# State-space mixer: one decay matmul for four heads, the gate, the root and the low parts a slot later, and four blocks begun at the end

## The chip, the core and the metric

The kernel runs on one core of one Trainium2 chip. The metric is the time of one execution in microseconds of device time. Before the change three runs gave 1684.92 us as median (1684.12 to 1685.75).

## The reference

Two transformer-like stacks run one behind the other on 256 tokens of width 1024 (16 meta tokens in front make it 272 in the first stack). The change touches the first layer alone, the state-space mixer. Cut to that:

```python
def ssd_mixer(h, w_in, conv_w, conv_b, dt_bias, a_log, d_skip, norm_g, w_out):
    zxbcdt = h @ w_in
    z, xbc, dt = jnp.split(zxbcdt, [SSD_D_INNER, SSD_D_INNER + SSD_CONV_DIM], axis=-1)
    xbc = jax.nn.silu(causal_depthwise_conv(xbc, conv_w, conv_b))
    xs, b_in, c_in = jnp.split(xbc, ...)
    dt = jax.nn.softplus(dt + dt_bias)
    ...
    a_cs = jnp.cumsum(a_dt, axis=-1)
    decay = jnp.exp(jnp.where(causal, a_cs[..., :, None] - a_cs[..., None, :], -jnp.inf))
    cb = jnp.einsum('bclgn,bcsgn->bcgls', c_c, b_c)
    y_diag = jnp.einsum('bcgjls,bcsgjp->bclgjp', cb[:, :, :, None] * decay, xdt)
    ...   # states carried from chunk to chunk, y_off from them
    y = y + xs * jnp.repeat(d_skip, SSD_HEAD_DIM)
    g = (y * jax.nn.silu(z)).reshape(bsz, L, SSD_GROUPS, SSD_D_INNER // SSD_GROUPS)
    g = g * lax.rsqrt(jnp.mean(g * g, axis=-1, keepdims=True) + EPS)
    return (g.reshape(bsz, L, SSD_D_INNER) * norm_g) @ w_out
```

There are 32 heads of 64 in 8 groups of 4, a state of 128, and a convolution of 4 taps. Behind the mixer come its MLP, an attention layer with its MLP, and the second stack; they are the same in both kernels.

## The kernel before, in words

All weights pass through as blocks of 128 output channels, in the order of one list, `PLAN`. Of each block of 128 x 1024 numbers SyncE loads the raw float32 (`RAW`, four slots), ScalarE makes the high part (`WH`, `act_split`), VectorE subtracts it to get the low part (`WL`, `dve_split`), and TensorE multiplies: for each of 8 chunks three matmuls, high by high, high by low, low by high (`pe_chunks`). A slot of `WH` is free again when TensorE has finished the block four places before. ScalarE splits three blocks ahead, VectorE two.

The mixer has 48 input blocks, six for each head group: two of x, one of B, one of C, two of the gate z. The code of each engine is written out in the order in which it runs: for each block n there stand the block's own work (split, convolution, SiLU) and then the steps of head groups that are due, which `ssd_cores` gives as pairs (g, k) with k = n - 6g - 5. So k counts the block at which a step of group g is issued, and one table, spread over `pe_ssd_core`, `act_ssd_core`, `dve_ssd_core` and `pool_ssd`, decides on every engine what is done at which k. For a convolved block ScalarE makes the base (scaled by tap 3, plus bias), VectorE adds three taps from the PSUM bank, ScalarE makes the tanh, and VectorE the SiLU from it.

A group is worked on in three tiles of tokens, 16, 128 and 128 wide. For each there are:

- `pe_prepare`: the product of B and C, transposes, and the running decay sums of the four heads laid over all partitions. The latter are four matmuls with a selector column (`DSEL`) as broadcast weights and the decay rows (`ACS`: 32 rows of high parts, 32 of low ones) as moving operand.
- `act_prepare`: exponentials of the sums (`CE`, for the part from the carried state) and of the differences (`EE`), and a copy of B transposed.
- GpSimd (`pool_ssd`): `CE` times C, in place, for tiles 1 and 2. It is the only GpSimd work of a round.
- `dve_prepare`, `dve_weigh`, `pe_apply`, `dve_take`: the masked product, the weighting by the decay, the products with x and the state, the sum with the skip term.

When the three tiles are through, the group is gated (VectorE, one instruction over 544 elements), squared (ScalarE), summed over channels (TensorE, `pe_group_sums`, two matmuls with ones), and its root is taken: ScalarE makes a rough one by logarithm and exponential, which needs a load of another function table and a load back (`act_table`), and VectorE corrects it by three Newton instructions (`dve_newton`). VectorE multiplies, ScalarE makes the high parts (`ASH`, `act_part`) and VectorE the low parts (`ASL`) which the output projection reads.

In the output projection (`ssdo`) row 0 takes chunks of groups 0 to 3 and row 1 those of groups 4 to 7, in 8 blocks each. While group 7 is still being worked on, `pe_ssd` begins the first three blocks of row 1 with the six chunks that are ready, and finishes them when group 7's low parts are there.

A name like pb stands for all PSUM banks, SCR for one large scratch tile in which most of the mixer's tiles are carved out. Below stand the functions that the change touches.

Of the kernel before, what the change touches and what calls it, by code (L numbers as in the profile page):

```python
# [22 lines left out]
for _n, _w in [("eps", 1), ("one", 1), ("lnmix", 16), ("ones", 128), ("ident", 128), ("tri", 128), ("convw", 128),  # L23
               ("convb", 32), ("dtb", 1), ("dsel", 32), ("alog", 1), ("ssdd", 16), ("ssdn", 16), ("lnmlp", 16),
               ("m384", 384), ("again", 384), ("past", 128), ("cmask", 128), ("sel2", 142), ("bdm", 128),
               ("i384", 1), ("i256", 1), ("rsel", 16), ("cs", 272), ("onerow", 256),
               ("qan", 3), ("kvan", 2), ("qn", 1), ("kn", 1), ("kn1", 1), ("memn", 8), ("ng", 96), ("gatb", 1),
               ("hg", 8)]:
    COLS[_n] = (_at, _w)
    _at += _w  # L30
# [171 lines left out]
def build_program(nc, cpack, xin, memin, W, out):  # L202
    with ExitStack() as ctx:
# [9 lines left out]
        def sig(name):  # L213
            sigs.append(Sig(sem(name)))
            return sigs[-1]
# [91 lines left out]
        def bank_of(i):  # L307
            name, r, m = PLAN[i]
            if name == "wqb":
                return banks[m // 2 % 2]  # L310
            return banks[3 if name == "mlao" and m == 3 else MEMBANK.get((name, m), i % 3)]

# [7 lines left out]
        def pe_bank_free(q, i):  # L320

            name, r, m = PLAN[i]
            if name == "wqb":
                if m > 3:
                    if m % 2 == 0:
                        q.wait_ge(*qsq[m // 2 - 2])
                else:
                    q.wait_ge(*eva[AT["wk", 0, 7]])
            elif name == "mlao" and m < 3:
                q.wait_ge(*qsq[7])  # L330
                q.wait_ge(*kw[15])
            elif name == "mlao" and m == 3:
                q.wait_ge(*ex[14])
            elif AT["ssd", 0, FIRST] <= i - 3 <= AT["ssd", 0, 47]:
                q.wait_ge(*ssd_read(i - 4))
            elif (name, m) in MEMBANK:
                for w in v_free(name, m):
                    q.wait_ge(*w)
            elif i > AT["mlin", 0, 23]:
                q.wait_ge(*evicted(max(j for j in range(i - 12, i) if bank_of(j) is bank_of(i))))  # L340
            elif i >= 3:
                q.wait_ge(*evicted(i - 3))
# [163 lines left out]
        ACS = sb("ACS", [64, T1], F32R)  # L506
        DSEL = sb("DSEL", [64, 32], F32R)
        halved = sig("conv_halved")
        spare = sig("spare_state_rows")
        xn, nh, nl = sig("x_normed"), sig("xn_high"), sig("xn_low")  # L510
# [29 lines left out]
        def ssd_cores(n):  # L540

            c = [(g, n - 6 * g - 5) for g in range(8) if 1 <= n - 6 * g - 5 <= 13]
            return c[::-1] if n < 48 else c
# [26 lines left out]
        def pe_prepare(q, g, i):  # L570
# [16 lines left out]
            if p is not None:  # L587
                q.wait_ge(*rel[p])
            q.wait_ge(*acd["low"])
            for h in range(4):  # L590
                t = q.matmul(a[:, 128 * h:128 * h + L], DSEL[:, 4 * g + h:4 * g + h + 1].broadcast_to([64, 128]),
                             ACS[:, o:o + L], True, True)
            t.then_inc(*prep_a(g, i))

# [49 lines left out]
        def pe_ssd(q):  # L644
# [21 lines left out]
            for n in range(56, 61):  # L666
                for g, k in ssd_cores(n):
                    pe_ssd_core(q, g, k)
                if n < 59:
                    i = q.block("ssdo", 1, n - 56)  # L670
                    pe_bank_free(q, i)
                    q.wait_ge(*lo[i])
                    pe_chunks(q, i, T1, ax[8:16], 0, 6)
                    begun.append(i)
            for m in range(8):
                if m < 3:
                    pe_chunks(q, begun[m], T1, ax[8:16], 6, 8)
                else:
                    pe_block(q, "ssdo", 1, m, T1, ax[8:16])
                pe_feed(q, "mlp0", m, T1, rms["ssd", 7])  # L680
# [17 lines left out]
        def act_dt_core(q, k):  # L698
            b = banks[3]
            q.wait_ge(*dtp[k])  # L700
            if k == 0:
# [3 lines left out]
                t.then_inc(*dta("tok"))  # L705
                q.activation(DSEL[:, :], cc("dsel", 0, 32, 0, 64), ACT.Copy).then_inc(*aca("selectors"))
                q.wait_ge(*acd["scanned", 2])
                q.activation(ACS[0:32, :], dtT[0:32, 3, :], ACT.Copy).then_inc(*aca("high"))
            else:
# [3 lines left out]
                for i in range(2):  # L713
                    L = TILES[i][1]
                    q.wait_ge(*dtd["to_end", i])
                    q.activation(dte[0:L, i, :], dte[0:L, i, :], ACT.Exp).then_inc(*dta("dte", i))

        def act_prepare(q, g, i):
# [26 lines left out]
        def act_ssd_core(q, g, k):  # L745
# [12 lines left out]
            elif k == 5:  # L758
                act_prepare(q, g, 2)
            elif k == 9:  # L760
                for c in range(2):
                    q.wait_ge(*gated[g])
                    q.activation(SQ[:, 2 * s + c, 0:T1], YB[:, s, c, :], ACT.Square).then_inc(*square(key, c))
            elif k == 11:
                act_table(q, key, row(RG0 + s, T1), T1, 256, vrow[g - 2, 1] if g > 1 else None)
# [22 lines left out]
        def act_ssd(q):  # L788
# [28 lines left out]
            for m in range(8):  # L817
                for g, k in ssd_cores(48 + m):
                    act_ssd_core(q, g, k)
                act_block(q, "ssdo", 0, m, T1)  # L820
            for n in range(56, 61):
                for g, k in ssd_cores(n):
                    act_ssd_core(q, g, k)
# [96 lines left out]
        def dve_ssd_core(q, g, k):  # L920
# [16 lines left out]
            elif k == 8:  # L937
                dve_take(q, g, 2)
                q.wait_ge(*ytake[g, 2])
                q.wait_ge(*silu[6 * g + 5])  # L940
                q.stt(y[:, :, :], y[:, :, :], 0.5, G6[:, g % 3, 4:6, :], ALU.mult, ALU.mult).then_inc(*gated(g))
            elif k == 12:
                dve_newton(q, key, row(RG0 + s, T1), SUMS[:, 0:T1], 256, rough[key])
            elif k == 13:
                q.wait_ge(*rms[key])
                if g:
                    q.wait_ge(*al["ssd", 2 * g - 1])
                for c in range(2):
                    q.tt(TMP[:, 6 + c, 0:T1], y[:, c, :], row(RG0 + s, T1), ALU.mult).then_inc(*vrow(g, c))
                for c in range(2):  # L950
                    q.wait_ge(*ah["ssd", 2 * g + c])
# [38 lines left out]
        def dve_ssd(q):  # L990
# [30 lines left out]
            for m in range(8):  # L1021
                for g, k in ssd_cores(48 + m):
                    dve_ssd_core(q, g, k)
                dve_x(q, "ssdo", 0, m, (s_x[m // 2], 16))
            dve_split(q, AT["ssdo", 0, 7] + 1)
            for n in range(56, 61):
                for g, k in ssd_cores(n):
                    dve_ssd_core(q, g, k)
# [6 lines left out]
        def pool_ssd(q):  # L1035
            q.wait_ge(s_cp[0], 16)
            q.ts(cc("convw"), cc("convw"), 0.5, ALU.mult).then_inc(*halved("w"))
            q.ts(cc("convb"), cc("convb"), 0.5, ALU.mult).then_inc(*halved("b"))
            q.mset(btk[:, 0, :], 0.0).then_inc(*spare("btk"))
            q.mset(xdd[:, 0, :], 0.0).then_inc(*spare("xdd"))  # L1040
            for n in range(61):
                for g, k in ssd_cores(n):
                    if k in (2, 5):
                        i = 1 if k == 2 else 2
                        o, L = TILES[i]
                        C4 = CE[:, :].rearrange("p (h l) -> p h l", h=4)
                        q.wait_ge(*cex[g, i])
                        q.tt(C4, C4, bc(G6[:, g % 3, 3, o:o + L], 4), ALU.mult).then_inc(*cem(g, i))
            for m in range(8):
# [2090 lines left out]
```

## Time and profile before

| | |
|---|---|
| median of three runs | 1684.92 us |
| the profiled execution | 1685.0 us |
| its span | 1683.2 us |
| TensorE busy (matmuls) | 1636.7 us, 97% |
| VectorE busy | 1172.2 us, 70% |
| ScalarE busy | 955.5 us, 57% |
| GpSimd busy | 365.5 us, 22% |
| share of the chain that ended last | PE 77%, DVE 10%, ACT 6%, issue 4% |
| granted clock of TensorE, mean | 0.996 |

The chain that ended last is followed back from the last instruction, so where two engines keep each other busy it shows the one on which the other waited. A busy TensorE is not one at its peak: matmuls are pipelined, and their ends are modelled, so the time between the starts of two of them is what one costs. In the mixer VectorE is at nine tenths of its time and more; behind it, from about 285 us on, TensorE runs nearly without a gap.

### The profile page before, as it was taken

The numbers are of one execution on the slowest core, as the hardware profiler recorded it, in microseconds if no ns is written. First come the engines' busy times: TensorE is split into PE (matmuls) and PEld (weight loads), VectorE is DVE, ScalarE is ACT, GpSimd is POOL, SyncE is SP. The second block draws the span as 40 slices with busy tenths as digits, with TensorE's granted clock in tenths as the row PEclk, the third lists the DMA queues.
The fourth block names the chain that finished last, engine by engine and source line by source line (L and its number), as shares of the span: only waits on it lengthen the run. The fifth ranks groups of instructions, "written<-read, shape, count | busy, mean of one in ns | idle before, by whom it ended". The sixth has DMA issues, their size and how long they took to land.

```text
span 1683.2 us, 32480 instructions
## 1 busy us (share of the span) xinstructions
PE 1636.7 (97%) x13066; PEld 1580.2 (94%) x13066; DVE 1172.2 (70%) x1967; ACT 955.5 (57%) x1741; POOL 365.5 (22%) x335
## 2 busy tenths in 40 slices
PE   7999999999999999999999999999999999999997
PEld 6998889999997889999999999999999998899996
DVE  7999987555567765555776656766688867576666
ACT  6677775544455666444756545644466765454443
POOL 0100011243351222444501202000251121100025
PEclk9999999999999999999999999999999999999999
DMA  5433334555542246555534534555564444445553
GB/s 196 138 117 110 121 107 137 167 173 185 173 136 82 76 137 202 188 184 188 168 128 161 178 124 154 172 171 183 181 192 152 138 143 133 139 136 167 182 183 110
DMA packets 76325, 257.26 MB, mean 153 GB/s; under 512 B 8464, under 2 KB 12560, under 8 KB 76048
## 3 DMA queue, kind: packets, MB, share of 16 engines
q1 hardware_dynamic: 76176, 255.19, 47.3%
q8 instruction: 104, 1.70, 0.4%
q14 instruction: 45, 0.37, 0.1%
HBM read 254.11 MB, written 1.05 MB: 152 GB/s over the span
## 4 chain that ended last, share of the span: by engine, by line
PE 77%; DVE 10%; ACT 6%; issue 4%; POOL 2%; DMA 0%; POOLq 0%; DVEq 0%; SPq 0%; ACTq 0%
PE pb L142 76%; DVE WL L161 3%; DVE TMP L173 2%; ACT SCR L151 2%; DVE SCR L173 2%; POOL X L161 1%; PE pb L145 1%; ACT WH L151 1%; ACT L158 1%; DVE SCR L161 1%; POOL SQ L161 1%; ACT ASH L151 1%; ACT TMP L151 0%; DVE HNL L173 0%; ACT SCR L152 0%
## 5 line engine op out<-in xcount | busy, mean ns | idle before, releaser
L161 DVE TENSOR_TENSOR WL<-RAW,WH 128x1024 fp32r<-128x1024 f32 (+4 forms) x514 | 605.1, 1179 | 17.1 <-ACT WH L151 16.9
L151 ACT ACTIVATE WH<-RAW 128x1024 fp32r<-128x1024 f32 (+4 forms) x514 | 507.6, 989 | 146.1 <-PE pb L142 143.5
L142 PE MATMUL pb<-HNH,WH 128*128 128x256 f32 (+1 forms) x1992 | 576.8, 290 | 6.3 <-issue 2.4
L142 PE MATMUL pb<-HNH,WL 128*128 128x256 f32 (+1 forms) x1992 | 565.1, 284 | 0.0
L142 PE MATMUL pb<-HNL,WH 128*128 128x256 f32 (+1 forms) x1992 | 564.9, 284 | 0.0
L142 PE MATMUL pb<-ASH,WH 128*128 128x256 f32 (+1 forms) x1560 | 449.2, 288 | 7.4 <-DVE WL L161 4.1
L142 PE MATMUL pb<-ASH,WL 128*128 128x256 f32 (+1 forms) x1560 | 443.2, 284 | 0.0
L142 PE MATMUL pb<-ASL,WH 128*128 128x256 f32 (+1 forms) x1560 | 442.6, 284 | 0.0
L142 PEld LDWEIGHTS pb<-HNH,WH 128*128 128x128 f32 x1992 | 375.8, 189 | 14.5 <-issue 4.9
L142 PEld LDWEIGHTS pb<-HNH,WL 128*128 128x128 f32 x1992 | 376.2, 189 | 0.0
L142 PEld LDWEIGHTS pb<-HNL,WH 128*128 128x128 f32 x1992 | 374.6, 188 | 1.2
L142 PEld LDWEIGHTS pb<-ASH,WH 128*128 128x128 f32 x1560 | 295.5, 189 | 12.0 <-issue 3.5
L142 PEld LDWEIGHTS pb<-ASH,WL 128*128 128x128 f32 x1560 | 295.4, 189 | 0.0
L142 PEld LDWEIGHTS pb<-ASL,WH 128*128 128x128 f32 x1560 | 294.7, 189 | 0.6
L161 POOL TENSOR_TENSOR SQ<-SQ 128x256 f32<-128x256 f32 (+1 forms) x61 | 80.1, 1314 | 213.8 <-ACT SQ L151 213.8
L142 PE MATMUL pb<-SCR 128*64 128x128 f32 (+10 forms) x880 | 120.4, 316 | 5.3 <-ACT SCR L151 2.5
L161 POOL TENSOR_TENSOR SCR<-SCR,TMP 128x256 f32<-128x256 f32 x46 | 56.5, 1229 | 309.9 <-DVE TMP L161 309.9
L161 DVE TENSOR_TENSOR ASL<-TMP,ASH 128x256 fp32r<-128x256 f32 (+1 forms) x108 | 46.5, 430 | 109.1 <-ACT ASH L151 109.1
L161 POOL TENSOR_TENSOR SCR<-SCR 128x512 f32<-128x512 f32 (+2 forms) x36 | 42.7, 1196 | 341.5 <-ACT SCR L151 231.8
L161 POOL TENSOR_TENSOR X<-X,TMP 128x272 f32<-128x272 f32 (+1 forms) x64 | 96.3, 1505 | 79.4 <-DVE TMP L161 79.4
L142 PEld LDWEIGHTS pb<-SCR 128*64 128x64 f32 (+4 forms) x880 | 90.0, 161 | 24.8 <-issue 7.9
L151 ACT ACTIVATE ASH<-TMP 128x256 fp32r<-128x256 f32 (+1 forms) x108 | 45.6, 422 | 117.1 <-DVE TMP L161 67.5
(158 smaller groups left out, 1805.6 us busy)
## 6 DMA issues: line engine op xcount, KB each, us to landing
RAW<-in_w_gu SPq DMA_DIRECT2D x88, 512.0 KB, 4.2
RAW<-in_w_up SPq DMA_DIRECT2D x64, 512.0 KB, 4.3
RAW<-in_w_down SPq DMA_DIRECT2D x64, 512.0 KB, 3.8
RAW<-in_w_ssd SPq DMA_DIRECT2D x48, 512.0 KB, 3.7
RAW<-in_w_xkv SPq DMA_DIRECT2D x32, 512.0 KB, 4.1
RAW<-in_w_mlin SPq DMA_DIRECT2D x24, 512.0 KB, 3.8
RAW<-in_w_fd SPq DMA_DIRECT2D x32, 384.0 KB, 3.1
RAW<-in_w_sbqkv SPq DMA_DIRECT2D x24, 512.0 KB, 3.7
```

What stands on the lines that cost most here:

```text
L142: return self.eng.matmul(o, l, r, start=start, stop=stop, skip_group_check=skip) if self.eng else Nothing()
L145: return self.eng.transpose(o, i, ident) if self.eng else Nothing()
L151: return self.eng.activation(o, i, f, bias=bias, scale=scale)
L158: self.eng.preload_act_table_set(name)
L161: return self.eng.tensor_tensor(o, a, b, op) if self.eng else Nothing()
L173: return self.eng.scalar_tensor_tensor(out=o, in0=a, scalar=s, in1=b, op0=op0, op1=op1)
```

## The change

It does five things.

1. **Decay operand.** `DSEL` becomes 128 x 8, one column for each group that marks the group's heads. A new tile `HROW` (128 partitions, 4 x 272) holds for each h of 0 to 3 the decay rows of those heads alone whose number within the group is h, and zero elsewhere; its upper 64 partitions are cleared by GpSimd at the start, and its lower 64 are written by four ScalarE copies with a mask as scale, once. One matmul per tile then does what four did.
2. **Slots.** The gate goes from k = 8 to 9, the squares from 9 to 10, the rough root from 11 to 12, the Newton steps from 12 to 13 (into the slot of the products), the low parts from 13 to 14. The group sums on TensorE stay at k = 11, the high parts on ScalarE at 13.
3. **GpSimd.** Its product for tile 1 also waits for the SiLU of block 6g + 6.
4. **Begun blocks.** Four blocks of row 1 are begun ahead, the fourth in PSUM bank 6.
5. **Splits.** ScalarE and VectorE split one weight block more before the last slots, whose number grows by one.

```diff
-               ("convb", 32), ("dtb", 1), ("dsel", 32), ...
+               ("convb", 32), ("dtb", 1), ("dsel", 12), ...
...
+            if (name, r, m) == ("ssdo", 1, 3):
+                return banks[6]
...
+            elif (name, r, m) == ("ssdo", 1, 3):
+                q.wait_ge(*sta1[7])
...
-        DSEL = sb("DSEL", [64, 32], F32R)
+        DSEL = sb("DSEL", [128, 8], F32R)
+        HROW = sb("HROW", [128, 4, T1], F32R)
...
-            c = [(g, n - 6 * g - 5) for g in range(8) if 1 <= n - 6 * g - 5 <= 13]
+            c = [(g, n - 6 * g - 5) for g in range(8) if 1 <= n - 6 * g - 5 <= 14]
...
-            q.wait_ge(*acd["low"])
-            for h in range(4):
-                t = q.matmul(a[:, 128 * h:128 * h + L], DSEL[:, 4 * g + h:4 * g + h + 1].broadcast_to([64, 128]),
-                             ACS[:, o:o + L], True, True)
-            t.then_inc(*prep_a(g, i))
+            q.wait_ge(*aca["rows"])
+            q.wait_ge(*hclear[0])
+            q.matmul(a[:, :].rearrange("p (h l) -> p h l", h=4)[:, :, 0:L], DSEL[:, g:g + 1].broadcast_to([128, 128]),
+                     HROW[:, :, o:o + L], True, True).then_inc(*prep_a(g, i))
...
-                if n < 59:
+                if n < 60:
...
+                q.wait_ge(*acd["low"])
+                for h in range(4):
+                    t = q.activation(HROW[0:64, h, :], ACS[:, :].bitcast(F32), ACT.Copy, cc("dsel", 8 + h, 1, 0, 64))
+                t.then_inc(*aca("rows"))
...
-            elif k == 9:
+            elif k == 10:
                 for c in range(2):
                     q.wait_ge(*gated[g])
                     q.activation(SQ[:, 2 * s + c, 0:T1], YB[:, s, c, :], ACT.Square).then_inc(*square(key, c))
-            elif k == 11:
+            elif k == 12:
                 act_table(q, key, row(RG0 + s, T1), T1, 256, vrow[g - 2, 1] if g > 1 else None)
...
+            act_split(q, AT["ssdo", 0, 7] + 1)
...
                 dve_take(q, g, 2)
+            elif k == 9:
                 q.wait_ge(*ytake[g, 2])
...
-            elif k == 12:
+            elif k == 13:
                 dve_newton(q, key, row(RG0 + s, T1), SUMS[:, 0:T1], 256, rough[key])
-            elif k == 13:
...
+            elif k == 14:
                 for c in range(2):
                     q.wait_ge(*ah["ssd", 2 * g + c])
...
-            dve_split(q, AT["ssdo", 0, 7] + 1)
+            dve_split(q, AT["ssdo", 0, 7] + 2)
...
+            q.mset(HROW[64:128, :, :].bitcast(F32), 0.0).then_inc(*hclear(0))
...
                         q.wait_ge(*cex[g, i])
+                        if i == 1:
+                            q.wait_ge(*silu[6 * g + 6 if g < 7 else 47])
                         q.tt(C4, C4, bc(G6[:, g % 3, 3, o:o + L], 4), ALU.mult).then_inc(*cem(g, i))
```

VectorE, in a steady round, at the block where the short tile is prepared (SCR<-pb,SCR and SCR<-SCR, 16x256), between this and the next weight split:

```order
 L161 TENSOR_TENSOR SCR<-pb,SCR 16x256
 L161 TENSOR_TENSOR SCR<-SCR 16x256
+L173 SCALAR_TENSOR_TENSOR TMP<-pb,Rbuf 128x272
+L173 SCALAR_TENSOR_TENSOR TMP<-TMP,Rbuf 128x272
+L173 SCALAR_TENSOR_TENSOR Rbuf<-TMP,Rbuf 128x272
 L161 TENSOR_TENSOR TMP<-SCR,Rbuf 128x272 x2
-L173 SCALAR_TENSOR_TENSOR ASL<-TMP,cp,ASH 128x272 x2
 L161 TENSOR_TENSOR WL<-RAW,WH 128x1024
 L173 SCALAR_TENSOR_TENSOR SCR<-TMP,pb 128x272
```

The three Newton instructions come in front of the products of the same group, and the low parts leave for the block behind.

ScalarE, in the same rounds, where it squares the gated group (SQ<-SCR) among base (TMP<-pb,cp), tanh (TMP<-TMP) and weight split:

```order
 L151 ACTIVATE TMP<-TMP 128x272
 L151 ACTIVATE SCR<-pb 128x256
+L151 ACTIVATE WH<-RAW 128x1024
+L151 ACTIVATE TMP<-pb,cp 128x272
+L151 ACTIVATE TMP<-TMP 128x272
 L151 ACTIVATE SQ<-SCR 128x272 x2
 L151 ACTIVATE WH<-RAW 128x1024
-L151 ACTIVATE TMP<-pb,cp 128x272
-L151 ACTIVATE TMP<-TMP 128x272
-L151 ACTIVATE WH<-RAW 128x1024
```

The squares now stand behind the next block's split, base and tanh.

TensorE, where it prepares a full tile (transposes on line 145, then the decay product, then the next weight block):

```order
 L142 MATMUL pb<-SCR 128x128
 L145 MATMUL pb<-cp,SCR 128x128 x3
-L142 MATMUL pb<-ACS,DSEL 128x128 x4
+L142 MATMUL pb<-HROW,DSEL 128x512
 L142 MATMUL pb<-HNH,WH 128x272
 L142 MATMUL pb<-HNL,WH 128x272
```

Four matmuls of 128 columns are one of 512; all else on TensorE stays where it was up to the begun blocks.

## Rows read from the trace of the kernel before

**Rows 1.** Chain of waits, 45 to 100 us: start us, us, what

```profile
89.65 1.63 ACT SCR L151 x5
```

**Rows 2.** Timeline of TensorE, decay products of tile 1: start us, us, instruction

```profile
75.97 0.66 PE L142 MATMUL pb<-ACS,DSEL 64*128 64x128 f32 x4
...
102.66 0.66 PE L142 MATMUL pb<-ACS,DSEL 64*128 64x128 f32 x4
```

**Rows 3.** Timeline of TensorE, waits in steady rounds, [idle before <-releaser]

```profile
130.39 0.39 PE L142 MATMUL pb<-HNH,WH 128*128 128x272 f32 x1 [0.30 <-DVE SCR L173]
...
158.25 0.39 PE L142 MATMUL pb<-HNH,WH 128*128 128x272 f32 x1 [0.30 <-DVE SCR L173]
...
166.07 0.39 PE L142 MATMUL pb<-HNH,WH 128*128 128x272 f32 x1 [0.53 <-DVE TMP L173]
```

**Rows 4.** Timeline of VectorE, root, weight split, products and low parts

```profile
149.97 0.44 DVE L173 SCALAR_TENSOR_TENSOR TMP<-pb,Rbuf 128x272 f32<-128x272 f32 x1 [0.59 <-ACT Rbuf L151]
...
151.28 1.22 DVE L161 TENSOR_TENSOR WL<-RAW,WH 128x1024 fp32r<-128x1024 f32 x1
...
153.85 0.78 DVE L161 TENSOR_TENSOR TMP<-SCR,Rbuf 128x272 f32<-128x272 f32 x2
155.79 0.50 DVE L173 SCALAR_TENSOR_TENSOR ASL<-TMP,cp,ASH 128x272 fp32r<-128x272 f32 x1 [1.17 <-ACT ASH L151]
```

**Rows 5.** Timeline, GpSimd's product beside the gate, beside the taking, and the gate alone

```profile
161.20 1.27 POOL L161 TENSOR_TENSOR SCR<-SCR 128x512 f32<-128x512 f32 x1 [13.85 <-ACT SCR L151]
...
161.33 1.72 DVE L173 SCALAR_TENSOR_TENSOR SCR<-SCR 128x544 f32<-128x544 f32 x1
...
229.63 1.29 POOL L161 TENSOR_TENSOR SCR<-SCR 128x512 f32<-128x512 f32 x1 [11.44 <-ACT SCR L151]
...
229.78 0.60 DVE L173 SCALAR_TENSOR_TENSOR SCR<-SCR,cp,pb 128x128 f32<-128x128 f32 x2
...
267.98 0.72 DVE L173 SCALAR_TENSOR_TENSOR SCR<-SCR 128x544 f32<-128x544 f32 x1
```

**Rows 6.** Timeline of TensorE, decay products and what follows them

```profile
151.90 0.61 PE L142 MATMUL pb<-ACS,DSEL 64*128 64x16 f32 x4
...
171.43 0.66 PE L142 MATMUL pb<-ACS,DSEL 64*128 64x128 f32 x4
172.02 1.19 PE L142 MATMUL pb<-SQ,cp 128*128 128x272 f32 x4
172.84 0.49 PE L142 MATMUL pb<-HNH,WH 128*128 128x272 f32 x1
```

**Rows 7.** Timeline of TensorE, matmuls of the third begun block

```profile
277.03 0.29 PE L142 MATMUL pb<-ASH,WL 128*128 128x272 f32 x1
...
277.41 0.29 PE L142 MATMUL pb<-ASH,WL 128*128 128x272 f32 x1
```

**Rows 8.** Timeline of ScalarE behind the root

```profile
149.84 1.04 ACT L151 ACTIVATE WH<-RAW 128x1024 fp32r<-128x1024 f32 x1
...
153.90 0.39 ACT L151 ACTIVATE TMP<-pb 128x272 f32<-128x272 f32 x1
```

**Rows 9.** Timeline of TensorE, waits at the turn and at the end

```profile
239.61 0.49 PE L142 MATMUL pb<-SCR 128*128 128x128 f32 x2 [1.11 <-ACT SCR L151]
...
279.47 0.39 PE L142 MATMUL pb<-ASH,WH 128*128 128x272 f32 x1 [1.77 <-DVE ASL L173]
```

**Rows 10.** Busy time by stretch: PE, PEld, DVE, ACT, POOL, granted clock, DMA share

```profile
229.00:257.00 28.00, 25.79 (x199) 23.54 (x198) 18.98 (x42) 19.42 (x41) 3.15 (x2) 0.94 0.32 101
```

**Rows 11.** Timeline: fourth block of row 1 on TensorE, the fifth's weight split on VectorE

```profile
282.28 0.36 PE L142 MATMUL pb<-ASH,WH 128*128 128x272 f32 x1 [0.24 <-DVE WL L161]
...
282.86 1.23 DVE L161 TENSOR_TENSOR WL<-RAW,WH 128x1024 fp32r<-128x1024 f32 x1
```

**Rows 12.** Timeline of ScalarE, the squares and the tanh behind them

```profile
166.65 0.74 ACT L151 ACTIVATE SQ<-SCR 128x272 f32<-128x272 f32 x2
...
169.89 0.43 ACT L151 ACTIVATE TMP<-TMP 128x272 f32<-128x272 f32 x1 [1.09 <-DVE TMP L173]
```

More of the change, by code:

```diff
@@ L23 @@
 for _n, _w in [("eps", 1), ("one", 1), ("lnmix", 16), ("ones", 128), ("ident", 128), ("tri", 128), ("convw", 128),
-               ("convb", 32), ("dtb", 1), ("dsel", 32), ("alog", 1), ("ssdd", 16), ("ssdn", 16), ("lnmlp", 16),
+               ("convb", 32), ("dtb", 1), ("dsel", 12), ("alog", 1), ("ssdd", 16), ("ssdn", 16), ("lnmlp", 16),
                ("m384", 384), ("again", 384), ("past", 128), ("cmask", 128), ("sel2", 142), ("bdm", 128),
@@ L506, in build_program @@
         ACS = sb("ACS", [64, T1], F32R)
-        DSEL = sb("DSEL", [64, 32], F32R)
+        DSEL = sb("DSEL", [128, 8], F32R)
+        HROW = sb("HROW", [128, 4, T1], F32R)
         halved = sig("conv_halved")
+        hclear = sig("head_rows_cleared")
         spare = sig("spare_state_rows")
@@ L675, in pe_ssd @@
             for m in range(8):
-                if m < 3:
+                if m < 4:
                     pe_chunks(q, begun[m], T1, ax[8:16], 6, 8)
@@ L705, in act_dt_core @@
                 t.then_inc(*dta("tok"))
-                q.activation(DSEL[:, :], cc("dsel", 0, 32, 0, 64), ACT.Copy).then_inc(*aca("selectors"))
+                q.activation(DSEL[:, :], cc("dsel", 0, 8), ACT.Copy).then_inc(*aca("selectors"))
                 q.wait_ge(*acd["scanned", 2])
@@ L820, in act_ssd @@
                 act_block(q, "ssdo", 0, m, T1)
-            for n in range(56, 61):
+            act_split(q, AT["ssdo", 0, 7] + 1)
+            for n in range(56, 62):
                 for g, k in ssd_cores(n):
@@ L1024, in dve_ssd @@
                 dve_x(q, "ssdo", 0, m, (s_x[m // 2], 16))
-            dve_split(q, AT["ssdo", 0, 7] + 1)
-            for n in range(56, 61):
+            dve_split(q, AT["ssdo", 0, 7] + 2)
+            for n in range(56, 62):
                 for g, k in ssd_cores(n):
@@ L1038, in pool_ssd @@
             q.ts(cc("convb"), cc("convb"), 0.5, ALU.mult).then_inc(*halved("b"))
+            q.wait_ge(*halved["b"])
+            q.mset(HROW[64:128, :, :].bitcast(F32), 0.0).then_inc(*hclear(0))
+            q.wait_ge(*hclear[0])
             q.mset(btk[:, 0, :], 0.0).then_inc(*spare("btk"))
@@ L3104 @@
     put("dtb", f["ssd_dt_bias"][0][:, None])
-    put("dsel", np.concatenate([np.eye(32, dtype=np.float32)] * 2, 0))
+    head = np.arange(64) % 32
+    put("dsel", (head[:, None] // 4 == np.arange(8)[None, :]).astype(np.float32))
+    put("dsel", (head[:, None] % 4 == np.arange(4)[None, :]).astype(np.float32), 8)
     put("alog", f["ssd_a_log"][0][:, None])
```

## Prediction

> **What bounds the kernel now.** I read the chain of waits first, then the time of single instructions in a round of the mixer, then the busy time by stretch. The change touches only the state-space mixer, the first 285 us of the span. One round is six weight blocks and one head group. In the chain TensorE's matmuls carry nearly everything up to 89 us; from there ScalarE and VectorE take over [rows 1]. The rounds tell the same. The decay products of tile 1 start 26.69 us apart in the second round [rows 2]; the first matmul behind the same product is 27.86 us apart from the fourth on [rows 3]. So TensorE alone needs 26.7 us for a round, and ScalarE and VectorE need 27.86: TensorE uses up the lead it had and then waits twice a round, for a SiLU (0.30 us) and for a convolution tap (0.53 us) [rows 3]. These idle times count from the modelled end of the matmul before; the difference of the periods, 1.17 us, is what they really cost, and four rounds have the pair (from 130, 158, 186 and 214 us). VectorE has two long idle times in a round, both waits for ScalarE: 0.59 us for the rough root, 1.17 us for the high parts [rows 4]. All else is VectorE work, one piece of it stretched: the gate, 544 elements wide, takes 1.72 us where GpSimd's product runs beside it, and 0.72 us where none does [rows 5].
>
> **The decay operand.** A head group has three tiles, each now with four matmuls of one head, afterwards with one for the four heads. For a full tile the four occupy TensorE from 171.43 to the next product at 172.02, 0.59 us, and four short ones are 0.05 us shorter as a group, 0.61 for 0.66, so 0.54 us [rows 6]. Eight times the columns add next to nothing: what is paid is four weight loads. The new matmul streams 512 columns. At the rate of the block matmuls, three of 272 columns in 0.38 us or 0.47 ns a column [rows 7], that is 0.24 us; I add 0.06 us until the next can start and take 0.30, which is 0.29 less than before. The bounds: 0.24 us with nothing added (0.35 saved), and the rate of plain float32, where two products of 272 columns take from 172.02 to 172.84 [rows 6], 0.41 us each, so 0.77 us for 512 columns, 0.83 with the same 0.06 (0.24 lost). I stay with the block matmuls, because operand and selector keep the type that runs as one instruction each today. The Trainium skill ("TensorE: Matmul & The Clock Gate", section "Back-to-back issue gap") gives a lone matmul of 512 columns 216 ns; with it the sum would be 0.4 us better over the 16 full tiles. The short tile streams 64 columns and stays at a weight load, a quarter of 0.54 and the same margin, 0.18 us: 0.36 less (bounds 0.2 and 0.4). A round saves 2 x 0.29 + 0.36 = 0.94 us of TensorE, seven rounds 6.6 us. TensorE's own period becomes 26.7 - 0.94 = 25.8 us.
>
> The new rows cost four ScalarE copies of 272 columns at about 40 us, 1.7 us if each is like a tanh of as many columns, 0.43 us [rows 12]. Behind them in ScalarE's queue stand the split of a weight block, which VectorE wants only a block later, and a tanh that waits for a tap anyway. So I take 0; without that cover it is 1.7 us. GpSimd clears the unused half at the start, long before a reader; 0.
>
> **Gate, root and low parts.** Each moves by one slot. The low parts no longer stand right behind the high parts that ScalarE makes: the 1.17 us go. The root was ready at 149.95; now a weight split and a tanh stand in front of it on ScalarE (1.06 and 0.33 us), so 151.35. VectorE was there at 149.38; now it has the split and the prepare first (2.57 - 0.13 us from 151.28 to 153.85), so 151.8 [rows 4, 8]: the 0.59 us go, by little. The SiLU behind the second table load needs a tanh that ScalarE ends at 154.3, after the same work as before [rows 8]; VectorE comes to it at 151.8 + 1.31 + 0.77 + 1.14 = 155.0. The gate leaves the block in which the product runs: 1.00 us back. VectorE's round, with a wait of 0.13 us for that tanh gone too, is then 27.86 - 1.17 - 0.59 - 0.13 - 1.00 = 25.0 us, under TensorE's 25.8. ScalarE now waits for products of the same block before it makes the high parts, but nothing of VectorE hangs on that until a block later.
>
> **GpSimd's product beside the taps.** It now waits for a SiLU as well, two blocks ahead of its reader. A tap reads one PSUM bank and one SBUF tile. No row shows taps under a product; the nearest is the pair that takes the output, operands of the same kinds, which lasts 0.60 us inside a product of 1.29 [rows 5]. So I take 0; were a tap held as the gate was, 1.0 us a round, VectorE's 26.0 would be 0.2 over TensorE's 25.8, 1.4 us in all. The Trainium skill ("SBUF — State Buffer", on the shared port pair) says that VectorE with two SBUF inputs and a GpSimd instruction that reads SBUF hold each other for the whole instruction. This speaks against the change only if the product starts late and outlasts the taps; the stretched gate above agrees with it.
>
> **Up to the last input block.** Four rounds lose 1.17 us of waiting, 4.7 us; seven rounds save 6.6 us: 11.3. I leave 0.15 us a round for small new waits: 10.2 us (bounds: 4.7 where the decay saving buys nothing, 11.3).
>
> **The turn to the output projection.** At 239.61 TensorE waits 1.11 us for a copy of the short tile [rows 9]. In front of the copy VectorE now has Newton steps (1.3 us) in place of low parts (0.8), and ScalarE its two high parts: about 0.6 us more. Group 7 saves 2 x 0.29 = 0.6 us right behind it. Together 0. In this stretch of 28 us the granted clock is 0.94 [rows 10], that is TensorE for a short time at 1.2 instead of 2.4 GHz, and 0.06 x 28 = 1.7 us lost, right after that wait. I leave it as it is.
>
> **The end.** TensorE waits from 277.54 to 279.47 for the low parts of group 7, 1.9 us, after three begun blocks [rows 7, 9]. A fourth begun block is 18 matmuls, 2.3 us, and covers it. The gate comes later, behind the splits, but still reaches the group sums within 0.1 us. What is late next is the fifth block's weights: their slot is free only when the first block is finished, and VectorE's split of them is done at 282.86 + 1.23 = 284.1 [rows 11], nothing in front of which gets sooner. Before, the fifth block starts behind the fourth's 24 matmuls from 282.28, at 285.3. So 1.1 us less, bounds 0 and 2.1.
>
> The sum is 10.2 + 0 + 1.1 = 11.3 us. The profiled execution took 1685.0 us, its span of 1683.2 and 1.8 around it; the median of the runs, 1684.92, is the same. 1685.0 - 11.3 = 1673.7.
>
> **Rivals.** A, the forecast: 1673.7. For it: TensorE alone set the second round.
> B: ScalarE and VectorE still set the pace, since the root or the tanh comes after VectorE does; the margins are only 0.45 and 0.7 us. With a period of 26.7 the decay saving buys nothing: 4.7 + 1.1 = 5.8 us, 1679.2.
> C: the decay product streams at the float32 rate, 16 x 0.53 = 8.5 us worse than A: 1682.2. Against it: today's run as single instructions.
> D, slower: the squares. They move into ScalarE's next block, behind a tanh that waits for that block's taps. Today they end at 167.39 and the sums start at 172.02 [rows 6, 12]. Behind the tanh at 169.89 they end at 171.1; the gate in front of those taps adds 0.66 us, and TensorE arrives 0.29 us sooner. No cover is left if VectorE lags as it does today, and TensorE waits before every group sum. It decides from 1.6 us a round (11.3 / 7); at 2.2 us it is 15.4 - 11.3 = 4.1 us slower, 1689.1. Against it: where TensorE is the bound, VectorE lags less.
> E: the low clock. If the longer wait doubles it, 1.7 us more, 1675.4; if it goes, 1672.0. The Trainium skill ("TensorE: Matmul & The Clock Gate", "HAM oscillation") says that idle gaps bring the low clock back; the trace agrees in this place, 0.94 after a wait of 1.11 us.
>
> **Chances.** A 0.55, B 0.20, C 0.04, D 0.06, E 0.15. The measurement can tell 0.2%, 3.4 us. Below 1681.5 lie A, E and 0.17 of B: 0.87. Within: C and the rest of B, 0.07. Slower: D, 0.06. The range goes from 1670.5 (E's better side and the decay product's lower bound, 16 x 0.06 = 1.0, with 0.5 of my margin for waits) to 1681.0 (B with 0.25 us more a round).
>
> **What would show it.** Rounds 25.8 us apart, and no idle time of TensorE over 0.3 us between 50 and 220 us; a decay instruction 0.3 us ahead of the next; the gate at 0.72 us; no wait of VectorE for the high parts; at the end a wait for weights in place of that for the low parts. It is wrong if the rounds stay at 26.7 us or more, if TensorE waits for squares before the sums, or if a decay matmul occupies over 0.5 us.

## The result, and the profile after

The changed kernel takes 1667.2 us (median of four runs, 1667.09 to 1667.49), the kernel before, measured beside it, 1684.79 (1684.12 to 1685.75). The ratio is 0.9892, with a 95% interval of 0.988 to 0.9904. The profiled execution took 1667.16 us with a span of 1665.4, against 1685.0 and 1683.2. So 17.6 to 17.9 us are gained where 11.3 were forecast; the time lies 3.3 us below the range.

The whole gain is made in the mixer: aligned by VectorE's weight splits, the two traces are 17.88 us apart at about 295 us of the changed kernel, and stay within 0.1 us of that to the end. Here is the page, first busy times, then the chain that ended last.

```profile
PE 1621.9 (97%) x12994; PEld 1570.9 (94%) x12994; DVE 1164.0 (70%) x1967; ACT 957.1 (57%) x1745; POOL 366.4 (22%) x336
...
PE 84%; DVE 6%; ACT 3%; issue 3%; POOL 2%; DMA 0%; POOLq 0%; SPq 0%; DVEq 0%; ACTq 0%
```

TensorE's part of the chain grows from 77% to 84%. The rounds show why: the time from one group's decay product to the next group's is the length of a round. This is TensorE's timeline of the changed kernel, the decay products of tile 1 [rows 2]:

```profile
74.12 0.48 PE L142 MATMUL pb<-HROW,DSEL 128*128 128x512 f32 x1
...
99.19 0.48 PE L142 MATMUL pb<-HROW,DSEL 128*128 128x512 f32 x1
...
149.33 0.48 PE L142 MATMUL pb<-HROW,DSEL 128*128 128x512 f32 x1
...
174.39 0.48 PE L142 MATMUL pb<-HROW,DSEL 128*128 128x512 f32 x1
...
199.47 0.48 PE L142 MATMUL pb<-HROW,DSEL 128*128 128x512 f32 x1
```

Every round from the second on takes 25.07 us, where before they took 26.7 and then 27.86, and the timeline has no wait of TensorE between 50 and 218 us. Both waits of a round [rows 3] are gone. By stretches (columns: busy time and instructions of PE, PEld, DVE, ACT, POOL, then the granted clock, the DMA share and GB/s), a steady round and a little more, the turn and the end of the mixer:

```profile
144.00:172.00 28.00, 28.00 (x242) 26.36 (x241) 26.93 (x59) 23.51 (x49) 2.58 (x2) 1.00 0.45 142
215.00:243.00 28.00, 24.00 (x201) 22.31 (x200) 21.12 (x44) 19.01 (x42) 4.31 (x3) 1.00 0.30 95
243.00:271.00 28.00, 26.55 (x213) 25.88 (x213) 20.99 (x37) 16.19 (x27) 2.83 (x3) 1.00 0.43 136
```

TensorE is busy for all 28.00 us of the first row, and VectorE for 26.93 of them, so VectorE has little in reserve. VectorE's timeline in that round shows the waits of [rows 4] gone, the product, the low parts and the gate [rows 5]:

```profile
147.02 0.80 DVE L161 TENSOR_TENSOR TMP<-SCR,Rbuf 128x272 f32<-128x272 f32 x2
...
152.34 0.91 DVE L173 SCALAR_TENSOR_TENSOR ASL<-TMP,cp,ASH 128x272 fp32r<-128x272 f32 x2
...
153.17 1.22 DVE L161 TENSOR_TENSOR WL<-RAW,WH 128x1024 fp32r<-128x1024 f32 x1
...
154.66 1.56 DVE L173 SCALAR_TENSOR_TENSOR TMP<-pb,cp,TMP 128x269 f32<-128x269 f32 x3
...
157.02 0.72 DVE L173 SCALAR_TENSOR_TENSOR SCR<-SCR 128x544 f32<-128x544 f32 x1
```

None of these carries an idle time in brackets; the one wait of VectorE left in the round is 0.22 to 0.26 us for TensorE, at the short tile. The gate takes 0.72 us instead of 1.72. The three taps take 1.56 us, as long as the round's other taps, although GpSimd's product now runs from 154.88 to 156.16 beside them.

Now the waits that are left, from TensorE's timeline: two at the turn and one at the end [rows 9, 11].

```profile
218.29 0.34 PE L142 MATMUL pb<-SCR 128*64 128x128 f32 x2 [1.99 <-DVE SCR L161]
...
225.12 0.38 PE L142 MATMUL pb<-SCR 128*128 128x128 f32 x1 [2.01 <-ACT SCR L151]
...
267.42 0.36 PE L142 MATMUL pb<-ASH,WH 128*128 128x272 f32 x1 [1.45 <-DVE WL L161]
```

The wait for group 7's low parts is gone, and the fifth block's weights come late in its place. Both waits at the turn (from the last input blocks to the output projection) have grown, from 1.10 (at 233.05) and 1.11 us.

### The profile page after: what moved, and what is told of

It is laid out like the page before. It is cut to its first block, busy times and chain, and to the rows that moved or that the text cites. A ratio compares the mean times of both kernels' runs of the same rounds, so it can differ in the third digit from the quotient of the medians.

```text
span 1665.4 us, 32342 instructions
## 1 busy us (share of the span) xinstructions
PE 1621.9 (97%) x12994; PEld 1570.9 (94%) x12994; DVE 1164.0 (70%) x1967; ACT 957.1 (57%) x1745; POOL 366.4 (22%) x336
## 4 chain that ended last, share of the span: by engine, by line
PE 84%; DVE 6%; ACT 3%; issue 3%; POOL 2%; DMA 0%; POOLq 0%; SPq 0%; DVEq 0%; ACTq 0%
PE pb L142 83%; DVE WL L161 2%; PE pb L145 1%; POOL X L161 1%; DVE TMP L173 1%; DVE SCR L173 1%; ACT SCR L151 1%; POOL SQ L161 1%; ACT WH L151 1%; ACT ASH L151 0%; ACT SCR L152 0%; DVE SCR L161 0%; DVE HNL L173 0%; ACT SQ L151 0%; DVE MX L182 0%
## 5 line engine op out<-in xcount | busy, mean ns | idle before, releaser
L161 DVE TENSOR_TENSOR WL<-RAW,WH 128x1024 fp32r<-128x1024 f32 (+4 forms) x514 | 604.2, 1177 | 17.9 <-ACT WH L151 17.6
```

Source lines behind the costliest of these rows:

```text
L161: return self.eng.tensor_tensor(o, a, b, op) if self.eng else Nothing()
```

## The experiments

They were measured in three sets, each beside the kernel before, whose medians there were 1684.43, 1685.18 and 1685.05 us. The changed kernel's 1667.2 is from the first measurement. The edits are against the changed kernel unless said otherwise, and keep all of the computation.

### Why a decay product is cheaper than forecast

TensorE saved 1.62 us a round (26.69 to 25.07) where I had 0.94. The profile shows where, if one takes the time from the last transpose before a decay product to the second matmul behind it. TensorE's timeline, first of the kernel before (the last of the three transposes starts at 102.46), then of the changed one (the last starts at 149.30):

```profile
102.24 0.49 PE L145 MATMUL pb<-cp,SCR 128*128 128x128 f32 x3
102.66 0.66 PE L142 MATMUL pb<-ACS,DSEL 64*128 64x128 f32 x4
103.25 0.39 PE L142 MATMUL pb<-HNH,WH 128*128 128x272 f32 x1
103.48 0.28 PE L142 MATMUL pb<-HNL,WH 128*128 128x272 f32 x1
```

```profile
149.08 0.49 PE L145 MATMUL pb<-cp,SCR 128*128 128x128 f32 x3
...
149.65 0.28 PE L142 MATMUL pb<-HNH,WH 128*128 128x272 f32 x1
149.76 0.29 PE L142 MATMUL pb<-HNL,WH 128*128 128x272 f32 x1
```

Before, 1.02 us pass; after, 0.46. The four matmuls themselves were 0.59 us, but 0.20 lay in front of them, where the changed kernel has 0.03, and 0.23 between the two block matmuls behind them, where it has 0.12. Without a decay product the transpose and the first block matmul would take about 0.11 and 0.12 us of this, the ordinary distances; so the product itself cost about 0.79 us before and 0.23 after. The view of weight loads shows what TensorE did there; before, and then after:

```profile
102.66 0.52 PEld L142 LDWEIGHTS pb<-ACS,DSEL 64*128 64x128 f32 x4 [0.17 <-issue]
```

```profile
149.30 0.19 PEld L142 LDWEIGHTS pb<-HROW,DSEL 128*128 128x128 f32 x1
149.41 0.19 PEld L142 LDWEIGHTS pb<-HNH,WH 128*128 128x128 f32 x1
```

Before, the load of a selector with 64 rows starts only 0.20 us after the start of the last transpose, with the loader idle for 0.17 us; afterwards the load of one with 128 rows starts together with the last transpose, and the next one 0.08 us after the start of the decay product, under it. Two kernels take the height and the number apart.

**One matmul, 64 rows.**

```diff
-        HROW = sb("HROW", [128, 4, T1], F32R)
+        HROW = sb("HROW", [64, 4, T1], F32R)
...
-            q.matmul(..., DSEL[:, g:g + 1].broadcast_to([128, 128]), HROW[:, :, o:o + L], ...)
+            q.matmul(..., DSEL[0:64, g:g + 1].broadcast_to([64, 128]), HROW[:, :, o:o + L], ...)
```

> The changed kernel, but operand and selector of the decay product have 64 partitions only (no cleared half); still one matmul for four heads. Theory 1 (height of the weights): a matmul whose weights fill 64 rows cannot have them loaded under the running 128-row one, nor the next 128-row weights under it, so the 0.2 us on entering and leaving come back: about 0.26 us a tile, 0.8 us a round, rounds of 25.85 us instead of 25.07, time 1673. Theory 2 (number of matmuls): what the forecast lacked comes from having one matmul in place of four, whatever its height: rounds stay at 25.07 us, time 1667.

Measured: 1674.94 us (1673.72 to 1675.98), ratio 0.9939 (0.9921 to 0.9956); rounds of 26.05 us. TensorE's timeline and its weight loads in it:

```profile
153.26 0.50 PE L142 MATMUL pb<-HROW,DSEL 64*128 64x512 f32 x1
153.69 0.39 PE L142 MATMUL pb<-HNH,WH 128*128 128x272 f32 x1
153.92 0.29 PE L142 MATMUL pb<-HNL,WH 128*128 128x272 f32 x1
```

```profile
153.26 0.18 PEld L142 LDWEIGHTS pb<-HROW,DSEL 64*128 64x128 f32 x1 [0.17 <-issue]
153.69 0.19 PEld L142 LDWEIGHTS pb<-HNH,WH 128*128 128x128 f32 x1 [0.24 <-issue]
```

The last transpose starts at 153.06. With the same number of matmuls and columns, 0.86 us pass where 128 rows need 0.46: the 64-row load starts 0.20 us after the start of the last transpose, and the next one only 0.43 us after the start of the 64-row matmul. So the height is worth 0.40 us for a full tile. The period was expected at 25.85 us, 0.2 less than measured.

**Four matmuls, 128 rows.**

```diff
-            q.matmul(a[:, :].rearrange("p (h l) -> p h l", h=4)[:, :, 0:L], ..., HROW[:, :, o:o + L], ...)
+            for h in range(4):
+                t = q.matmul(a[:, 128 * h:128 * h + L], ..., HROW[:, h, o:o + L], ...)
```

> The changed kernel, but four matmuls for each tile again, one of each head, all with 128-row operand and selector. Theory 1 (height): entering takes 0.03 us and leaving 0.11 as in the changed kernel, only four weight loads of 0.11 stand where one matmul of 0.32 was: about 0.15 to 0.2 us a tile, rounds of 25.6 us, time 1671. Theory 2 (number): all of the saving is lost, rounds of 26.7 us, time 1679.

Measured: 1671.8 us (1671.32 to 1673.4), ratio 0.992 (0.9899 to 0.994); rounds of 25.82 us, 0.68 us for a full tile. The number alone is worth 0.22 us there; and of the 1.02 us before, 0.34 goes with the height alone. For the short tile, where 0.75 us pass before, 0.44 with one matmul of 64 rows, 0.56 with four of 128 and 0.25 in the changed kernel, the number is worth more (0.31) than the height (0.19). Over a round, taken one at a time from the changed kernel, the height is worth 0.98 us and the number 0.75: both theories had a part, the height the larger one.

### Each half of the change by itself

**The kernel before with the decay operand alone** (slots, GpSimd's wait and begun blocks as before).

> The kernel before with the new decay operand alone. If ScalarE and VectorE set the pace of the steady rounds, these stay at 27.86 us and TensorE only waits longer (about 2.8 us a round): time 1682 to 1684. Rival: TensorE's saving counts by itself, 8 groups by 1.6 us: time 1672.

Measured: 1681.64 us (1680.66 to 1684.22, ten runs), ratio 0.9981 (0.9972 to 0.999). The rounds are 27.85 us from the third on, the old period of the later rounds, and the saving has turned into waits. TensorE's timeline of one round:

```profile
123.60 0.39 PE L142 MATMUL pb<-HNH,WH 128*128 128x272 f32 x1 [0.60 <-DVE SCR L173]
...
128.72 0.39 PE L142 MATMUL pb<-HNH,WH 128*128 128x272 f32 x1 [1.05 <-DVE SCR L173]
...
136.54 0.40 PE L142 MATMUL pb<-HNH,WH 128*128 128x272 f32 x1 [0.54 <-DVE TMP L173]
```

**The changed kernel with the old decay product** (four matmuls with `ACS` and the 64-row selector, no `HROW`).

> The changed kernel with the old decay product (four matmuls of 64 rows). If the moved slots take VectorE and ScalarE off the critical path, TensorE alone sets rounds of 26.7 us from the second on: 11.3 us more than the changed kernel over seven rounds and about 1 for group 7, time 1679. Rival (slots matter only where TensorE is fast): rounds of 27.86 us, time 1685.

Measured: 1679.56 us (1677.12 to 1681.35, eight runs), ratio 0.9967 (0.9956 to 0.9978). The rounds are 26.69 us without a wait from 50 to 228 us: TensorE's own old period. Its eight runs spread over 4.2 us, and the shortest have the highest granted clock: 1677.1 and 1677.3 us at 0.997, 1680.2 to 1681.4 at 0.993 and 0.994. Alone the halves give 2.8 and 4.9 us (7.2 by the two runs at 0.997; this half has the fourth begun block too), together 17.6: each takes away one of two bounds that lie 1.2 us apart, and only both let the period fall to 25.07.

### The slots, one by one

**Low parts back at k = 13**, behind the products.

```diff
-            elif k == 14:
                 for c in range(2):
                     q.wait_ge(*ah["ssd", 2 * g + c])
```

> The changed kernel with the low parts back at k = 13, right behind the high parts. Theory 1 (the wait for the high parts is the dear one): VectorE is busy 26.93 of 28 us in the changed kernel, 24.1 of a round of 25.07; a wait of about 1.2 us or more for ScalarE comes back in each round and does not fit, so the rounds become 25.8 to 26.5 us and TensorE waits for SiLU or tap, time 1672 to 1677. Rival: VectorE has slack enough, rounds stay at 25.07, time 1667.

Measured: 1676.36 us (1674.74 to 1678.79), ratio 0.9944 (0.9928 to 0.996); rounds of 26.76 us. VectorE's timeline, then TensorE's:

```profile
150.91 0.92 DVE L173 SCALAR_TENSOR_TENSOR ASL<-TMP,cp,ASH 128x272 fp32r<-128x272 f32 x2 [0.97 <-ACT ASH L151]
```

```profile
153.37 0.39 PE L142 MATMUL pb<-HNH,WH 128*128 128x272 f32 x1 [1.43 <-DVE SCR L173]
```

VectorE's wait for the high parts is back, and TensorE waits 1.43 us for the SiLU behind it, once a round; the period is even a little above the expected range. This slot is worth the most, 9.2 us by the medians and 7.7 by the profiled runs.

**The gate back at k = 8, GpSimd's product without its wait for a SiLU.**

```diff
-            elif k == 9:
                 q.wait_ge(*ytake[g, 2])
...
-                        if i == 1:
-                            q.wait_ge(*silu[6 * g + 6 if g < 7 else 47])
```

> The changed kernel with the gate back at k = 8 and GpSimd's product without the wait for the SiLU, so both are in one block again. Theory 1 (every us of VectorE counts): the gate takes 1.72 us again, VectorE's round is 25.1 us or more, rounds of 25.1 to 25.8, time 1668 to 1672. Rival (only the order against ScalarE mattered): rounds 25.07, time 1667.

Measured: 1675.67 us (1674.85 to 1677.34), ratio 0.9942 (0.9925 to 0.9958); rounds of 26.50 us with one wait for a tap. TensorE's timeline:

```profile
133.88 0.39 PE L142 MATMUL pb<-HNH,WH 128*128 128x272 f32 x1 [1.17 <-DVE TMP L173]
```

More than I had expected of the two together, so I took them apart.

**The product without its wait, the gate at k = 9.**

> The changed kernel with the gate at k = 9 as changed, but GpSimd's product without the wait for the SiLU. Theory 1 (a product held against two-input VectorE work costs wherever it falls): it runs in block 1 of the round beside the low parts, which are held for about 1 us, so the rounds grow to 25.5 us or more, time 1670 to 1673. Theory 2 (only the gate, in front of the taps that TensorE waits for, is worth moving): rounds stay within 25.1 to 25.3, time 1667 to 1668.5.

Measured: 1670.9 us (1670.2 to 1672.96), ratio 0.9921 (0.9904 to 0.9937); rounds of 25.76 us. GpSimd's timeline and VectorE's:

```profile
154.10 1.42 POOL L161 TENSOR_TENSOR SCR<-SCR 128x512 f32<-128x512 f32 x1 [11.28 <-ACT SCR L151]
```

```profile
153.89 1.92 DVE L173 SCALAR_TENSOR_TENSOR ASL<-TMP,cp,ASH 128x272 fp32r<-128x272 f32 x2
```

The product ends at 155.52 and the low parts beside it at 155.81: 1.92 us for the pair instead of the 0.91 above. TensorE then waits 0.46 us for a tap (at 158.83). With its wait the product runs beside taps, and these take no longer for it.

**The gate at k = 8, the product with its wait.**

> The changed kernel with the gate back at k = 8, but the wait of GpSimd's product kept, so the gate runs without a product beside it. Theory 1 (the holding is what counts, not the place): rounds of 25.07, time 1667. Theory 2 (the place before the taps counts): 0.66 us more in front of the taps that TensorE waits for, rounds of 25.4 to 25.8, time 1669 to 1672.

Measured: 1671.11 us (1669.9 to 1673.06), ratio 0.9919 (0.9904 to 0.9934); rounds of 25.51 us. Nothing stretches the gate here, and still it costs 0.44 us a round: at k = 8 its 0.7 us stand in front of the taps for which TensorE waits (0.16 us at 106.25), at k = 9 it stands behind the taps of that block. Place and overlap cost 0.44 and 0.69 us a round alone and 1.43 with both, more than their sum.

**The root and the Newton steps back at k = 11 and 12.**

```diff
-            elif k == 12:
+            elif k == 11:
                 act_table(q, key, row(RG0 + s, T1), ...)
...
-            elif k == 13:
+            elif k == 12:
                 dve_newton(q, key, row(RG0 + s, T1), SUMS[:, 0:T1], 256, rough[key])
+            elif k == 13:
```

> The changed kernel with the rough root back at k = 11 on ScalarE and the Newton steps back at k = 12 on VectorE. Theory 1: VectorE waits again for the rough root, 0.6 us or more a round, and there is 0.3 us of slack: rounds of 25.3 to 25.7 us, time 1669 to 1672. Rival: this step alone buys nothing, time 1667.

Measured: 1665.9 us (1665.03 to 1668.64), ratio 0.9883 (0.9869 to 0.9898). Not slower. The last rounds before the turn are longer, 25.3 to 25.5 us with waits up to 0.38, and VectorE waits 0.59 us for the root again; but at the turn TensorE waits 1.44 and 0.63 us instead of 1.99 and 2.01. The whole time flatters this kernel a little: its record has no low-clock stretch in the attention, where the changed one has one of 1.7 us. Up to 298 us of the changed kernel, where each has had one such stretch, it is 0.6 us ahead. So the later root buys nothing in sum.

### The end, and two better versions

**Three begun blocks**, with the splits of before.

```diff
-                if n < 60:
+                if n < 59:
...
-                if m < 4:
+                if m < 3:
```

> The changed kernel with three begun blocks and the splits of before. If the fourth block covers the wait for the low parts and the fifth block's weights are the next limit, the wait for the low parts (1.8 us) is back and that of 1.45 us for weights goes: 1.1 us more than the changed kernel, time 1668.3. Rival: the fourth block only moves the wait, 1667.

Measured: 1667.45 us (1667.21 to 1669.71), ratio 0.9899 (0.9884 to 0.9914). By the time alone the fourth block is worth 0.25 us, less than these runs can tell. But this kernel has one low-clock stretch behind the mixer and none at 42 us, the changed one has both. From the preparation of group 7's last tile (238.59 us with three, 239.11 with four) to the same weight split of VectorE behind the mixer (274.85 and 274.51) neither has such a stretch: 36.26 and 35.40 us, so the fourth block is worth 0.86. TensorE's timeline with three:

```profile
261.92 0.39 PE L142 MATMUL pb<-ASH,WH 128*128 128x272 f32 x1 [1.77 <-DVE ASL L173]
...
264.74 0.36 PE L142 MATMUL pb<-ASH,WH 128*128 128x272 f32 x1 [0.24 <-DVE WL L161]
```

So 1.77 and 0.24 us of waits become the one of 1.45 us.

**Newest group first also in blocks 48 and 49, the fifth block's weights split sooner.**

```diff
-            return c[::-1] if n < 48 else c
+            return c[::-1] if n < 50 else c
...
+                if m == 0:
+                    act_split(q, i + 1)
...
+                if m == 1:
+                    dve_split(q, AT["ssdo", 1, 2])
```

> The changed kernel with two edits: head groups newest first also in blocks 48 and 49, so that the short tile of group 7 is prepared before the last tile of group 6 is applied and before group 5's Newton steps; and the weights of the fifth block of row 1 split one step sooner. If the waits of 1.99 and 2.01 us at the turn hang on the order, they shrink to under 2 us together, and that of 1.45 us at the end to under 0.5: 2 to 4 us less than the changed kernel, time 1663 to 1665. Rival: the waits hang on ScalarE's chain with two table loads and only move, 1666 to 1668.

Measured: 1666.48 us (1665.92 to 1667.08), ratio 0.9884 (0.9869 to 0.9899). TensorE's timeline:

```profile
218.75 0.20 PE L142 MATMUL pb<-SCR 128*16 128x16 f32 x2 [1.43 <-DVE SCR L173]
...
223.93 0.49 PE L142 MATMUL pb<-SCR 128*128 128x128 f32 x2 [0.23 <-ACT SCR L151]
...
229.33 1.04 PE L142 MATMUL pb<-SCR 16*64 16x16 f32 x10 [1.25 <-DVE SCR L173]
...
266.40 0.36 PE L142 MATMUL pb<-ASH,WH 128*128 128x272 f32 x1 [0.30 <-DVE WL L161]
```

The wait at the end shrinks from 1.45 to 0.30, those at the turn from 4.0 to 1.66, but a new one of 1.25 appears, and three low-clock stretches are in its record instead of two. The time lies in the rival's range and not in the 1663 to 1665 expected of the new order: at the turn the waits have in part only moved.

**Root and Newton steps at k = 11 and 12 for groups 5 to 7, and the sooner split.**

```diff
-            elif k == 12:
+            elif k == (11 if g >= 5 else 12):
                 act_table(q, key, row(RG0 + s, T1), ...)
```

> The changed kernel with two edits: for the groups from 5 on the rough root and the Newton steps stay one slot sooner (11 and 12), since with them all sooner the two waits at the turn were 1.44 and 0.63 us instead of 1.99 and 2.01; and the fifth block's weights split one step sooner, as in the run before (0.30 us of wait instead of 1.45). If both add up, the time is about 3 us under the changed kernel, 1664, with the low clock in as many stretches. Rival: the waits come back elsewhere, as one of 1.25 us did in the run with the groups newest first, 1666 to 1667.

Measured: 1665.3 us (1664.01 to 1665.97), ratio 0.9883 (0.9868 to 0.9897). TensorE's timeline:

```profile
217.77 1.26 PE L142 MATMUL pb<-SCR 128*64 128x128 f32 x18 [1.98 <-DVE SCR L161]
...
223.23 0.49 PE L142 MATMUL pb<-SCR 128*128 128x128 f32 x2 [0.64 <-ACT SCR L151]
...
264.38 0.36 PE L142 MATMUL pb<-ASH,WH 128*128 128x272 f32 x1 [0.30 <-DVE WL L161]
```

The four runs lie below all four of the changed kernel, by about 2 us where 3 were expected. The intervals of the ratios overlap, so this is the fastest version seen, not one proven faster.

## Why the prediction was wrong in size

The direction and the mechanism, rival A, were right: TensorE alone sets the rounds. The step that failed is **the decay operand**, a term of the sum that was mis-sized.

**The decay operand.** I took "what is paid is four weight loads" and set 0.59 us against 0.30. From the new matmul's start to the next 0.32 us pass, near the 0.30; but its start is recorded 0.03 us behind that of a transpose which takes 0.11, so what it adds is 0.23, the bound I had with nothing added. The larger error was before: I read only the time between the first of the four and what follows, and left out what their 64 rows do to the neighbours, so 0.59 us stood for about 0.79 (0.20 us in front where a transpose takes 0.11, 0.23 behind where a block matmul takes 0.12). Measured, a full tile saves 0.56 us instead of 0.29, the short one 0.51 instead of 0.36 (a quarter of 0.54 with the margin of 0.06 is 0.20 and not the 0.18 I wrote, so 0.34 by my own terms), a round 1.62 instead of 0.94. Over seven rounds that is 4.8 us, with group 7's two full tiles 0.5 more, and its short tile, 0.5 us, was in no term of my sum. The rows were in the trace of before: [rows 6] alone do not show it, but the weight loads beside them (0.17 us idle) and the 0.23 us after the next matmul do. Bounding the price by the product's own rows was the error; the pair of kernels with 64 and 128 rows shows the cause.

**The rounds.** The 4.7 us of waits are gone, as forecast, and the halves show that they go only with the slots. The 0.15 us a round that I left for new waits, 1.1 us in the sum, were not needed. VectorE was forecast at 25.0 us a round. The record shows 26.93 busy in 28, or 24.1 in a round of 25.07, though some of its waits lie in the rest, so the reserve is small.

**The slots.** The waits for the high parts and the root are gone. Of the root's step the runs say that in sum it was not needed. Of the gate I had only the stretch, 1.00 us; its place was worth 0.44 us a round by itself. The product beside taps costs 0, as taken. So do the copies into `HROW`, which take 1.76 us of ScalarE from 39.90 on. The first prepare does start later in the changed kernel, but there the low-clock stretch at 42.5 us lies just in front of it; the kernel with three begun blocks has the same copies and no such stretch. TensorE's timelines at this place, of the kernel before, of the changed one, and of that with three begun blocks:

```profile
45.35 0.20 PE L142 MATMUL pb<-SCR 128*16 128x16 f32 x2 [0.81 <-DVE SCR L173]
```

```profile
45.88 0.23 PE L142 MATMUL pb<-SCR 128*16 128x16 f32 x2
```

```profile
45.39 0.20 PE L142 MATMUL pb<-SCR 128*16 128x16 f32 x2 [0.80 <-DVE SCR L173]
```

So 0.5 us of delay come with the low clock and 0.04 at most with the copies.

**The turn.** I expected the second wait to grow by 0.6 us, and the first was not in my account. They grew by 0.89 and 0.90. Two things have a part: with the decay operand alone, where all slots are the old ones, they are already 1.66 and 1.73 us, since TensorE needs less time and VectorE and ScalarE do not; and with root and Newton steps in their old slots the two are 1.9 us shorter together. The low clock of [rows 10] did not come here (1.00 from 215 to 243 us) although both waits were longer, so the wait of 1.11 us before it was not shown to be its cause. A stretch came at 42.5 us instead, beside the one that both kernels have in the attention. Windows of before, and of after (columns as above, the clock third from the end):

```profile
241.00:245.00 4.00, 4.00 (x21) 4.00 (x21) 3.64 (x9) 2.24 (x8) 1.00 (x1) 0.57 0.38 131
546.00:554.00 8.00, 7.08 (x42) 6.74 (x43) 5.70 (x17) 4.11 (x13) 1.72 (x2) 0.79 0.18 51
```

```profile
40.00:48.00 8.00, 6.77 (x43) 6.49 (x44) 7.89 (x15) 6.98 (x16) 0.00 (x0) 0.79 0.47 140
528.00:536.00 8.00, 7.02 (x43) 6.65 (x42) 5.62 (x18) 4.17 (x13) 1.72 (x2) 0.79 0.18 49
```

By 0.43 x 4 or 0.21 x 8 us each such stretch loses 1.7 us of TensorE's work. Each kernel has two; those in the attention cancel. The one at 42.5 us falls into a part where TensorE had time to spare (it waits 0.8 us there without it), and cost 0.5 us by the rows above, where that of 241 us cost the old kernel up to 1.7.

**The end.** 1.1 us were forecast, 0.9 were measured, and the wait for the fifth block's weights was the one named.

The account: rounds 11.3 (7 x 1.62) and 4.7; the two waits at the turn -1.8; the low-clock stretch that is gone from it 1.7; group 7's three tiles 1.6; the end 0.9; the later start under the low clock -0.5. Together 17.9, as seen. Forecast were 10.2, 0 and 1.1. The low-clock stretches are luck, some 1.2 us of the gain in these two records: no part of the change was meant to move them.

**The rivals.** B (the pair sets the pace, rounds of 26.7, 1679.2) is what the rounds are without the low parts' slot (26.76 us, 1676.36); the margins of root and tanh, on which B hung, held. C falls: 0.32 us for 512 columns, not 0.83. D falls: no wait before the group sums in any round. E's low clock moved rather than doubled.

## What to carry to other kernels

The price of a small matmul is not the time until the next one starts. Take the time from the last ordinary matmul before it to the second one behind it, and look at the weight loads in between: an idle time there tells of a cost that the neighbours pay. Where two bounds lie close, each edit alone gives little and both together much, so forecast the period as the larger of the engines' own, after all edits. When one engine gets faster and its partners do not, look for longer waits in the next stage.

## What the runs showed of the hardware

- At each change between 64 and 128 rows the next weight load started late, with the loader idle for 0.17 us before the 64-row load and 0.24 before the next 128-row one; with 128 rows throughout, the loads started 0.00 to 0.08 us behind the start of the matmul before. From the last transpose to the decay product it was 0.20 us against 0.03, between the two block matmuls behind 0.23 against 0.12, and from one 512-column matmul to the next 0.43 against 0.32.
- GpSimd's product over 512 elements held VectorE where it read and wrote only SBUF (the gate, 1.72 for 0.72 us; the low parts, 1.92 for 0.91), and not where one operand came from PSUM (taps 1.56 us for three, with and without). Beside the product of tile 2 a weight split of 1024 elements still takes 1.72 us instead of 1.22 in every round (at 165.42); no wait of TensorE follows it in the changed kernel's rounds.
- The low-clock stretches came in a few parts of the program, at 32 us, at 41 to 43, at 223 to 241 and at 504 to 549, and which of them had one differed between nearly equal kernels: the changed kernel has one at 42.5 us, the one with three begun blocks, the same program up to there, has none. The records have one to four before the end. What decides it, these runs do not show. A gain of under 2 us can be hidden or feigned by one of them: of the fourth begun block's 0.86 us the whole time shows 0.25.
